# One full-precision product inside each feed-forward block becomes two that accumulate

## The reference

```python
x = first_block(...)       # 2 layers: a wide projection, three kinds of mixing, an output projection
h = h + 0.5 * swiglu(rmsnorm_2(h, ffn1_norm), w_gate, w_up, w_down)      # first feed-forward, 2816 wide
h = h + mixing(h)          # attention, spatial gating, two gated branches, output projection
h = h + 0.5 * swiglu(rmsnorm_2(h, ffn2_norm), w_gate, w_up, w_down)      # second feed-forward
return rmsnorm_2(h, final_norm)

def swiglu(x, w_gate, w_up, w_down):
    return (jax.nn.silu(x @ w_gate) * (x @ w_up)) @ w_down
```

## Time and profile before

| | us |
|---|---|
| three runs | 1161.39, 1161.57, 1162.5 (median 1161.57) |
| the profiled execution | 1161.61 |
| its span, first to last instruction | 1159.8 |
| TensorE busy | 1144.5 (99%) |
| POOL busy | 835.6 (72%) |
| DVE busy | 695.2 (60%) |
| ACT busy | 655.1 (56%) |

### The profile page before, as it was taken

One profiled execution on the slowest core, in us unless ns is written; L12 is line 12 of the kernel. 1 busy time (PEld: TensorE's weight loads), 2 busy tenths in 40 slices (PEclk: granted clock), 3 DMA queues, 4 the chain that ended last, 5 costly groups with the idle time before them and its releaser, 6 DMA issues.

```text
span 1159.8 us, 22847 instructions
## 1 busy us (share of the span) xinstructions
PE 1144.5 (99%) x8974; PEld 1076.9 (93%) x8974; DVE 695.2 (60%) x1257; ACT 655.1 (56%) x1093; POOL 835.6 (72%) x1087
## 2 busy tenths in 40 slices
PE   8999999999999999999999999999999999999996
PEld 7788999999988899899999999999789999999996
DVE  5786644466578655356656555556767457555554
ACT  7666754575676587346656444446566447444443
POOL 6988798669598869877857656567756785755652
PEclk9999999999999999999999999999999999999998
DMA  8553344545454434444565554654533554655540
GB/s 309 185 172 129 121 171 168 178 153 203 154 180 158 170 110 164 170 164 164 184 225 200 194 190 173 209 180 148 178 132 128 207 198 142 219 182 201 181 164 37
DMA packets 64123, 199.89 MB, mean 172 GB/s; under 512 B 6608, under 2 KB 17936, under 8 KB 64016
## 3 DMA queue, kind: packets, MB, share of 16 engines
q1 hardware_dynamic: 62192, 195.31, 48.8%
q10 hardware_dynamic: 1824, 3.11, 0.8%
HBM read 196.57 MB, written 1.84 MB: 171 GB/s over the span
## 4 chain that ended last, share of the span: by engine, by line
PE 94%; DVE 2%; ACT 1%; POOL 1%; DMA 1%; issue 0%; ACTq 0%; DVEq 0%
PE ps L1620 51%; PE ps L1678 20%; PE ps L1668 13%; PE ps L1636 2%; PE ps L1830 2%; DVE ring L951 1%; PE ps L1924 1%; POOL ring L348 1%; PE ps L1904 1%; PE ps L1934 1%; DMA x<-in_x 1%; PE ps L1865 1%; PE ps L1925 0%; PE ps L2061 0%; PE ps L1804 0%; ACT xs L472 0%
## 5 line engine op out<-in xcount | busy, mean ns | idle before, releaser
L348 POOL TENSOR_TENSOR ring<-raw,ring 128x256 fp32r<-128x256 f32 x1032 | 807.6, 817 | 295.1 <-ACT ring L455 294.7
L1620 PE MATMUL ps<-xs,ring 128*128 128x256 f32 x5040 | 608.3, 280 | 0.4 <-POOL ring L348 0.3
L1620 PEld LDWEIGHTS ps<-xs,ring 128*128 128x128 f32 x5040 | 590.9, 188 | 9.1 <-issue 5.9
L455 ACT ACTIVATE ring<-raw 128x1024 fp32r<-128x1024 f32 x364 | 377.4, 1051 | 88.9 <-PE ps L1678 48.9
L1678 PE MATMUL ps<-ys,ring 128*128 128x256 f32 x2016 | 240.0, 279 | 0.0
L1678 PEld LDWEIGHTS ps<-ys,ring 128*128 128x128 f32 x2016 | 236.0, 188 | 0.0
L951 DVE TENSOR_TENSOR ring<-raw,ring 128x1024 fp32r<-128x1024 f32 x106 | 155.1, 1464 | 128.0 <-ACT ring L455 127.6
L1668 PE MATMUL ps<-ring,xs 128*128 128x512 f32 x672 | 165.7, 398 | 1.3 <-DVE ring L951 1.3
L1668 PEld LDWEIGHTS ps<-ring,xs 128*128 128x128 f32 x672 | 122.7, 188 | 30.4 <-issue 3.6
L785 ACT ACTIVATE ys<-ca 128x256 fp32r<-128x256 f32 x44 | 18.3, 417 | 113.4 <-DVE ca L1414 113.4
L1263 DVE SCALAR_TENSOR_TENSOR ca<-ps,par,ca 128x253 f32<-128x253 f32 (+2 forms) x96 | 46.0, 479 | 35.8 <-ACT ca L541 34.4
(11 more groups left out here) (270 smaller groups left out, 967.5 us busy)
## 6 DMA issues: line engine op xcount, KB each, us to landing
raw<-in_w SPq DMA_DIRECT2D x364, 512.0 KB, 3.4
y<-bias_rows SPq DMA_DIRECT2D x6, 256.0 KB, 4.3
out_y<-y SPq DMA_DIRECT2D x4, 256.0 KB, 2.5
const<-in_const SPq DMA_DIRECT2D x1, 896.0 KB, 10.5
x<-in_x SPq DMA_DIRECT2D x3, 256.0 KB, 7.3
bias_rows<-lg ACTq DMA_DIRECT2D x1, 768.0 KB, 7.0
dec<-in_wT ACTq DMA_DIRECT2D x1, 512.0 KB, 3.5
qke<-in_ln ACTq DMA_DIRECT2D x1, 512.0 KB, 4.5
```

The lines of the kernel that those rows point to most:

```text
L348: last = pool.tensor_tensor(ring[:, g % RING, 1, part], raw[:, g % RAW, part], ring[:, g % RING, 0, part].bitcast(F32), ALU.subtract)
L455: act.activation(ring[:, g % RING, 0, :], raw[:, g % RAW, :], ACT.Copy).then_inc(S["hi"], 1)
L1620: last = mm(ps[bank][:, half * T:(half + 1) * T], ring[:, slot % RING, wp, (at + k) * P:(at + k + 1) * P], rhs(k, xp), start=(first and i ...
```

## The change

The one product at PAUSE becomes a loop over two: the identity times the first 256 columns of the constants, then times the second 256, the first opening the sum in bank 0 and the second adding to it. Nothing else is different; it is done once in each of the two feed-forward blocks.

```diff
                     if f == PAUSE:
-                        mm(ps[2 * (f % 2)][:, 0:T], ident, const[:, 0:T], start=True, stop=True)
+                        for c in range(2):
+                            mm(ps[2 * (f % 2)][:, 0:T], ident, const[:, c * T:(c + 1) * T],
+                               start=(c == 0), stop=(c == 1))
                     tile_product(2 * (f % 2), 0, slot, xs_part).then_inc(S["slots_used"], 1)
```

## The result

The changed kernel took 1150.86 us, median of four runs (1150.65 to 1151.98), against 1161.86 for the kernel before in the same comparison: a ratio of 0.9906, interval 0.9894 to 0.9918. Forecast were 1149.9 us. The profiled execution took 1150.74 us, its span is 1148.9.

What follows compares the result with a forecast made beforehand. TensorE, busy 99% of the span, bounds the kernel: 0.86 for added products, -5.87 block 2, -6.22 block 1, -0.51 mixing make -11.74 from 1161.61, so 1149.9 us; range 1148.5 to 1157.2 (first case alone 1148.5 to 1151.5).

Steps and rivals of the forecast that it cites:

- TensorE is the bound, and the pace is where the time is: Whole kernel: TensorE busy 99% of the span; the same matmuls take 113.3 or 117.8 ns, slow steps 3.9% longer.
- The added product, 0.43 us each: At PAUSE in both feed-forward blocks: one more product per block, nothing hides it, +0.86 us in all.
- From the fast pace a pair returns to it, a single does not: At PAUSE, block 2: entered fast, it stays fast behind two products, -5.89 us and +0.02 for the transition.
- rival 1: Both blocks: the pair does nothing to the pace, block 1 stays and block 2 falls slow; 1162.5 us, chance 0.10.
- the other bank: Objection at PAUSE: the pair writes the bank that the next product opens, which the sum of squares does not.
- not everything of four passes keeps the pace: Objection from full-precision work at 125.83 us: 24 matmuls take 2.74 us ahead of it and 2.83 behind.
- the phase that led out of the slow pace: Block 1 at PAUSE: passes of 377 or 378 ns, not 382, mean the pair makes it fast; -6.24 us, +0.02 transition.
- Rival 2: Only block 2 profits; the pair keeps block 1's slow pace as at 799.61 us; 1156.6 us, chance 0.18.
- it all comes earlier by the same amount: Mixing behind block 1: its DVE and ACT work follows TensorE's last results, so the whole gain is passed on.
- I see no new wait: Feed-forward blocks: 8.16 us steps can still be fed; POOL busy grows from 6.81 to 7.1 of 10 us.
- Rival 4: The mixing is left slow after a 0.43 us shift, block 2 stays slow; +3.1 us, 1165.6 us, chance 0.06.
- 112.4 ns: Mixing in the trace of before: 258 records in 29 us, read as TensorE leaving the mixing at the fast pace.

Runs made afterwards that it cites:

- third run of the changed kernel: The changed kernel measured a third time, unchanged: 1151.03 us, ratio 0.9923 against the kernel before; two of its six runs were 1157.07 and 1157.23.

## Why the prediction was right, and where not

**TensorE is the bound, and the pace is where the time is:** right. Block 2 gained 5.45 us against 5.44.

**The added product, 0.43 us each:** right to the hundredth, in both blocks.

**From the fast pace a pair returns to it, a single does not:** right: the pair kept it 56 times of 56, and the single product lost it 4 times of 4. Of the objections under rival 1, the other bank is answered (met fast, L1607 and PAUSE behave alike), and "not everything of four passes keeps the pace" was true for other shapes: 512 columns don't.

**Block 1, "the phase that led out of the slow pace":** this step was wrong, though the number came. The forecast had block 1 enter the pair slow and be led out by it, told by 377 against 382 ns. In the profile it enters fast, which the stall decided ahead of anything that was changed: for this step the number came by luck. When the pair does meet the slow pace, it leads out in 15 of 23 cases, and in none of 3 in the steps of block 1. The mark was read at the wrong place. The first pass of a single product lasts 377 in all seven cases, also in the block where a pair fails behind it. The 382 is the first pass of the pair itself: it stands in 7 of the 8 pairs that stayed slow and in none of the 71 that came out fast, so it goes with the outcome, and nothing ahead of the pair foretells it. Rival 2 (one block only, 1156.6 us) is, by the times, no rival but the other outcome of the same kernel: 1157.1 and 1157.2 in two of 14 runs. Its chance of 0.18 is near that by accident.

**The sum.** Against the forecast's -11.74 the profiled execution shows -10.87:

| term | forecast | measured |
|---|---|---|
| block 1, up to the sum of squares behind it, product included | -5.79 | -6.09 (799.61 to 793.52) |
| on to ACT's step in the mixing | -0.51 | -0.48 (813.65 to 807.08 is -6.57) |
| rest of the mixing | 0 | +1.20 (-6.57 to -5.37) |
| block 2, product included | -5.44 | -5.45 |

The four measured terms make -10.82; the other 0.05 are the rounding and the end of the chain.

Block 1 gained 0.3 us more, since the pace was fast ahead of the pair too. The mis-sized term is the mixing: "it all comes earlier by the same amount" was put at nothing and measured +1.2 us. It looked at the work of DVE and ACT behind TensorE's last results and left out POOL: 0.9 of the 1.2 are lost at DVE's subtraction, which ended with a burst of 40 that came 5.7 us earlier and not 6.6. That the feed was sufficient ("I see no new wait") held within both blocks.

**Rival 4** (the mixing left slow) didn't come as priced. Its mechanism exists in a smaller form: in 7 of the 13 profiles the matmuls ahead of the sum of squares of block 2 are slow, so the stalls in the mixing don't bring one pace about as the forecast argued. In the third run of the changed kernel the 192 matmuls of L1678 take 22.62 us there instead of 21.78, and from their start to the sum of squares it is 0.7 us more. The sum of squares then led out of it in six of the seven; in the seventh, the profile of four products, block 2 was entered slow. The 112.4 ns that the forecast reads in the earlier trace rows is a little low, since the count holds records that reach over the edges of the window; the chain has 264 matmuls in 30.14 us there, 114.2 ns each.

What stays open: what the slow pace is inside TensorE, what makes a pair lead out of it in one case and not in another, and what makes the stall near 618 us be left fast or slow.

## What to carry to other kernels

Where one engine is busy all the time, divide the pieces of its chain by their counts before looking for waits: a 4% difference in pace over 300 us is invisible in busy shares. Here it was worth some 11 us, when the longest single wait of TensorE in the kernel before was 1.8 us. Look then for what stands at the place where the pace changes, and for the same sequence elsewhere in the trace; earlier places told here what the pair would do when met fast, and did not tell what it would do when met slow. When an engine runs ahead, ask too which other engine's burst the next step waits for, and what sets the start of that burst. Run such a kernel often: one whose pace is decided at a stall can have two times, and a median of four doesn't show it.

## What the runs showed of the hardware that I had not expected

- A dense stream of matmuls of 256 columns runs at 113.3 or 117.8 ns each (8.16 or 8.48 us for 72), at a granted clock of 1.00 both times, and holds either pace for over a thousand matmuls. What was executed just before changes it; behind a stall, and behind a pair met slow, it came out either way.
- A full-precision product of 256 columns costs 0.43 us in two passes. Behind one the pace was always slow (7 of 7); behind two it was fast whenever it was fast ahead of them (56 of 56). One of 512 columns takes the time of two and acts like one.
- At one place a subtraction on DVE, of which the next one took 1.23 us, took 8.5 to 9.5 us within a burst of 40 subtractions on POOL (27.9 us without a pause), and ended 1.1 us behind POOL's last in all 13 profiles. At 616.18 us in the trace of before one took 1.70 us within a burst of 16.
